# A hybrid decoder trunk on one core: GpSimd's order in the mixing stage, the places of the preparation groups, the order at a stage's first residual, and x and the output in fewer transfers

## What is computed

```python
for l in range(2):
    x = x + 0.5 * swiglu(rmsnorm(x, norm_ffn1[l]), ffn1_w_in[l], ffn1_w_out[l])   # width 2816
    z = rmsnorm(x, norm_mix[l]) @ mix_w_in[l]                                      # 1024 -> 1536
    y_ssm = s5_group(z[:, 0:512], ...)       # diagonal complex state space model, 32 groups
    y_gm = gmlp_group(z[:, 512:1024], z[:, 1024:1536], gm_v_gain[l], gm_w_s[l], gm_b_s[l])
    y = concatenate([rmsnorm(y_ssm, gain_ssm_out[l]), rmsnorm(y_gm, gain_gm_out[l])])
    x = x + y @ mix_w_out[l]
    x = x + 0.5 * swiglu(rmsnorm(x, norm_ffn2[l]), ffn2_w_in[l], ffn2_w_out[l])
return rmsnorm(x, norm_final)
# gmlp_group: u, v = gelu(u), gelu(v); v = rmsnorm of each head of v, times v_gain
#             out = u * (tril(w_s) @ v + b_s), in chunks of 128 tokens
```

## Time and profile before

| | us |
|---|---|
| median of 3 runs | 996.69 (996.29 to 998.61) |
| the profiled execution, its own time | 996.66 |
| its span | 994.9 |
| PE busy in the span | 955.3 |

### The profile page before, as it was taken

The page is one execution under the profiler, slowest core; times in us unless marked ns, Lnnn a source line. Parts: engine busy times, 40 slices in busy tenths (PEclk is TensorE's granted clock), DMA queues, the critical chain, the costliest instruction groups (busy, mean ns, idle before and its releaser), DMA issues.

```text
span 994.9 us, 12027 instructions
## 1 busy us (share of the span) xinstructions
PE 955.3 (96%) x4639; PEld 800.0 (80%) x4639; DVE 553.4 (56%) x619; ACT 470.2 (47%) x670; POOL 391.7 (39%) x611
## 2 busy tenths in 40 slices
PE   5999999999799999999899999999997999999996
PEld 4888888888698888888788888888887888888885
DVE  4556664357657555664256555544684665555543
ACT  5544443456346445443255544443654464544442
POOL 6789998654500788998550000000242000000001
PEclk9999999999899999999799999999997999999999
DMA  9865555344225756554345656555532256556551
GB/s 241 241 199 170 178 197 176 127 130 167 94 77 169 216 178 193 180 191 156 120 126 180 198 177 197 180 187 193 169 127 85 75 180 190 190 169 213 189 169 43
DMA packets 128824, 165.10 MB, mean 166 GB/s; under 512 B 17144, under 2 KB 108416, under 8 KB 128768
## 3 DMA queue, kind: packets, MB, share of 16 engines
q1 hardware_dynamic: 128448, 163.78, 51.8%
q10 hardware_dynamic: 320, 0.56, 0.2%
HBM read 163.27 MB, written 1.05 MB: 165 GB/s over the span
## 4 chain that ended last, share of the span: by engine, by line
PE 57%; POOL 29%; DVE 5%; issue 4%; ACT 2%; SPq 1%; DMA 1%; POOLq 0%; ACTq 0%; DVEq 0%
PE bank L344 16%; PE bank L346 16%; PE bank L345 16%; POOL pt L1080 8%; POOL sc L1080 7%; POOL sc L1083 4%; POOL bp L1080 4%; POOL cw L1086 2%; DVE w_lo L853 1%; PE bank L542 1%; PE bank L585 1%; PE bank L528 1%; PE bank L471 1%; ACT w_hi L647 1%; PE bank L398 1%
## 5 line engine op out<-in xcount | busy, mean ns | idle before, releaser
L853 DVE TENSOR_TENSOR w_lo<-raw,w_hi 128x1024 fp32r<-128x1024 f32 x304 | 383.4, 1265 | 349.6 <-ACT w_hi L647 349.3
L647 ACT ACTIVATE w_hi<-raw 128x1024 fp32r<-128x1024 f32 x304 | 321.2, 1061 | 307.6 <-PE bank L346 301.0
L344 PE MATMUL bank<-w_hi,x_hi 128*128 128x512 f32 x864 | 343.5, 398 | 1.3 <-DVE x_lo L868 1.3
L346 PE MATMUL bank<-w_hi,x_lo 128*128 128x512 f32 x864 | 337.6, 391 | 0.0
L345 PE MATMUL bank<-w_lo,x_hi 128*128 128x512 f32 x864 | 337.0, 390 | 0.0
L346 PEld LDWEIGHTS bank<-w_hi,x_lo 128*128 128x128 f32 x864 | 162.4, 188 | 34.8
L344 PEld LDWEIGHTS bank<-w_hi,x_hi 128*128 128x128 f32 x864 | 162.7, 188 | 33.3 <-issue 1.6
L345 PEld LDWEIGHTS bank<-w_lo,x_hi 128*128 128x128 f32 x864 | 162.9, 188 | 31.9
L1089 POOL TENSOR_TENSOR rstd_c<-ms_c,neg_half 128x2 f32<-128x2 f32 (+1 forms) x8 | 5.8, 724 | 411.4 <-DVE ms_c L873 411.3
L344 PE MATMUL bank<-w_hi,h_hi 128*128 128x512 f32 x352 | 139.4, 396 | 0.0
L345 PE MATMUL bank<-w_lo,h_hi 128*128 128x512 f32 x352 | 137.7, 391 | 0.0
(11 more groups left out here) (137 smaller groups left out, 709.9 us busy)
## 6 DMA issues: line engine op xcount, KB each, us to landing
raw<-in_ffn_w_in SPq DMA_DIRECT2D x174, 512.0 KB
raw<-in_ffn_w_out SPq DMA_DIRECT2D x44, 1024.0 KB
raw<-in_mix_w_in SPq DMA_DIRECT2D x12, 1024.0 KB
raw<-in_mix_w_out SPq DMA_DIRECT2D x8, 1024.0 KB
raw<-in_ffn_w_in SPq DMA_DIRECT2D x4, 256.0 KB, 3.6
x<-in_x SPq DMA_DIRECT2D x6, 128.0 KB, 4.9
out<-x SPq DMA_DIRECT2D x6, 128.0 KB, 2.7
ws_raw<-in_gm_w_s SPq DMA_DIRECT2D x2, 256.0 KB
```

Source lines behind the costliest of these rows:

```text
L344: mm(o, hi_a, hi_b, start=first, stop=False)
L346: return mm(o, lo_a, hi_b, start=False, stop=last)
L647: A(w_hi[:, n % RING, :], raw[:, s, (n % 2) * 1024:(n % 2) * 1024 + 1024], ACT.Copy).then_inc(hi_done, 1)
L853: TT(w_lo[:, n % RING, :], raw[:, s, (n % 2) * 1024:(n % 2) * 1024 + 1024], w_hi[:, n % RING, :].bitcast(F32), ALU.subtract).then_inc(lo_d ...
```

## The change

It reorders instructions on all engines and merges transfers. No arithmetic is added but one split of a small transpose in two; the last scaling of one quarter of x moves from GpSimd and ACT to DVE.

```diff
-GROUP_AT = (9, 12, 15, 18)
+GROUP_AT = ((9, 13, 16, 18), (11, 14, 16, 18))
...
@@ SP: x and the output (xv and ov are views (h, j, n, d) of x and out)
-            for j in range(T):
-                sp.dma_start(x[32 * j:32 * j + 32, 0, :], xv[0, j]).then_inc(x_full[0], 16)
-            for j in range(2):
-                sp.dma_start(x[32 * j:32 * j + 32, 1, :], xv[1, j]).then_inc(x_full[1], 16)
+            for c in range(2):
+                sp.dma_start(x[:, 0, c * 512:c * 512 + 512], xv[0, :, :, c * 512:c * 512 + 512]).then_inc(x_full[c][0], 16)
...
-            for j in range(T):
-                sp.dma_start(ov[0, j], x[32 * j:32 * j + 32, 0, :]).then_inc(stored, 16)
-            sp.wait_ge(fin_done[1], 2)
-            for j in range(2):
-                sp.dma_start(ov[1, j], x[32 * j:32 * j + 32, 1, :]).then_inc(stored, 16)
-            sp.wait_ge(stored, 2 * T * 16)
+            sp.dma_start(ov[0], x[:, 0, :]).then_inc(stored, 16)
+            sp.wait_ge(fin_done[1], 1)
+            sp.dma_start(ov[1, :, :, 0:512], x[:, 1, 0:512]).then_inc(stored, 16)
+            sp.wait_ge(stored, 3 * 16)
...
@@ PE: wide_half, the first block of the first stage
-                    if first_block and kt == 0:
-                        if hh == 0:
-                            x_turn(l, i, 1, 1)
+                    if first_block and kt == 0 and l + i:
+                        x_turn(l, i, 1, 1)
+                if first_block and hh == l + i == 0:
+                    x_turn(l, i, 1, 0)
+                    x_turn(l, i, 1, 1)
...
@@ PE: ffn, after input block b
                         if b == PREP_SMALL[f]:
                             prep_small(f, bank[2 * t1_])
+                        if f == b == 0:
+                            pe.wait_ge(gain_full, 16 * 4)
+                            nc.tensor.transpose(bank[2 * t1_ + 1][:, 0:GAINS], gain_rows,
+                                                ident[0:GAINS, 0:GAINS]).then_inc(gain_t, 1)
+                        if f == 0 and b == 1:
+                            pe.wait_ge(gain_done, 2)
...
-                    if f < DEPTH and k in GROUP_AT:
-                        n = GROUP_AT.index(k)
+                    if f < DEPTH and k in GROUP_AT[f]:
+                        n = GROUP_AT[f].index(k)
...
@@ ACT: first loads
+            act.dma_start(gain_rows[0:KT * DEPTH, :],
+                          a["norm_ffn1"].rearrange("l (t p) -> (l t) p", p=P)).then_inc(gain_first, 16)
+            for c in range(2):
+                act.dma_start(x[:, 1, c * 512:c * 512 + 512], xv[1, :, :, c * 512:c * 512 + 512]).then_inc(x_full[c][1], 16)
...
-            act.wait_ge(xg_done, 1)
-            act.wait_ge(rstd_done, 3 * DEPTH + 2)
-            act.wait_ge(sq_done, 12 * DEPTH + 4)
-            A(x[:, 1, 512:1024], xg, ACT.Copy, scale=rstd_c[:, 1:2]).then_inc(fin_done[1], 1)
             act.wait_ge(fin_done[1], 2)
-            for j in range(2, T):
-                act.dma_start(ov[1, j], x[32 * j:32 * j + 32, 1, :]).then_inc(stored, 16)
+            act.dma_start(ov[1, :, :, 512:1024], x[:, 1, 512:1024]).then_inc(stored, 16)
...
@@ DVE: norm_in; the loops over halves before it end one half earlier
-                    for c, t in ((0, 0), (0, 1), (1, 0)):
-                        residual(before, acc, pairs[c], last_half, c, t, scales[t])
+                    residual(before, acc, pairs[0], last_half, 0, 0, scales[0])
+                    split(l, h + 1)
+                    residual(before, acc, pairs[0], last_half, 0, 1, scales[1])
+                    residual(before, acc, pairs[1], last_half, 1, 0, scales[0])
...
@@ DVE: the last norm
-                if t == 0:
-                    dve.wait_ge(sq_done, 12 * DEPTH + 2)
-                    mean(3 * DEPTH, 0, 1)
-            dve.wait_ge(gfin_full, 16)
-            finish(0, 0)
+                    if c == 1 and t == 0:
+                        dve.wait_ge(sq_done, 12 * DEPTH + 2)
+                        mean(3 * DEPTH, 0, 1)
+                    if c == 0 and t == 1:
+                        finish(0, 0)
+            finish(1, 0)
             dve.wait_ge(sq_done, 12 * DEPTH + 4)
             mean(3 * DEPTH, 1, 2)
-            finish(1, 0)
             finish(0, 1)
+            finish(1, 1)
...
@@ POOL: mix
-                state(1)
                 pool.wait_ge(vms_done, l + 1)
                 inv_sqrt(vrs[:, :], vms[:, :], vrs_done)
-                pool.wait_ge(vrs_done, l + 1)
+                state(1)
+                pool.wait_ge(im_done, l * 2 + 2)
...
@@ POOL: the program's start
-                pool.wait_ge(gain_t, 1)
+                pool.wait_ge(gain_t, 2)
...
+            norm(norm_no(0, 0))
             prep_first(0)
-            norm(norm_no(0, 0))
             prep_rest(0)
```

More of the change, by code:

```diff
@@ L172, in build @@
         first_full = sem("first_full")
-        x_full = [sem("x_full0"), sem("x_full1")]
+        x_full = [[sem(f"x_full{c}{t}") for t in range(2)] for c in range(2)]
+        gain_first = sem("gain_first")
         small_full, c_full, late_full = sem("small_full"), sem("c_full"), sem("late_full")
@@ L243, in load_first @@
             def load_first(w_in, k):
-                src = w_in[0].rearrange("(t p) m -> p t m", p=P)
+                src = w_in[0].rearrange("(t p) (g m) -> p t g m", p=P, g=2)
                 dst = raw[:, 0, :].rearrange("p (t g m) -> p t g m", t=4, g=2)
-                for g in range(2):
-                    sp.dma_start(dst[:, 2 * k:2 * k + 2, g, :],
-                                 src[:, 2 * k:2 * k + 2, g * FF:g * FF + 256]).then_inc((first_full, raw_full[0])[k], 16)
+                for t in range(2 * k, 2 * k + 2):
+                    sp.dma_start(dst[:, t], src[:, t, :, 0:256]).then_inc((first_full, raw_full[0])[k], 16)
             def load_rows(l, c, w, k):
@@ L351, in x_turn @@
                 if l == 0 and i == 0:
-                    pe.wait_ge(x_full[h], 16 * T)
+                    pe.wait_ge(x_full[c][h], 16)
                 else:
@@ L658, in squares @@
                 if l + i == 0:
-                    act.wait_ge(x_full[t], 16 * T)
+                    act.wait_ge(x_full[c][t], 16)
                 else:
@@ L730, in ffn @@
                             prep_small(f, bank[2 * t1_])
+                            if f == 0:
+                                act.wait_ge(gain_t, 2)
+                                A(gains[:, KT * DEPTH:GAINS], bank[2 * t1_ + 1][:, KT * DEPTH:GAINS],
+                                  ACT.Copy).then_inc(gain_done, 1)
                         if h == 4 * PREP_SMALL[f] + 11:
@@ L817, in _ @@
                               a[name].rearrange("l (t p) -> (l t) p", p=P)).then_inc(gain_full, 16)
-            xv = a["x"][0].rearrange("(h n j) d -> h j n d", j=T, n=32)
-            for j in range(2, T):
-                act.dma_start(x[32 * j:32 * j + 32, 1, :], xv[1, j]).then_inc(x_full[1], 16)
             act.wait_ge(gain_t, 1)
-            A(gains[:, :], bank[0][:, 0:GAINS], ACT.Copy).then_inc(gain_done, 1)
+            A(gains[:, 0:KT * DEPTH], bank[0][:, 0:KT * DEPTH], ACT.Copy).then_inc(gain_done, 1)
             act.wait_ge(gain_done, 1)
@@ L920, in ffn @@
                     norm_in(l, 2, UPS[j], ACC_SSM, (ors[:, 2:3], ors[:, 3:4]), OUT + KT - 1)
-                for h in range(4, 4 * UB + FT + 2):
+                for h in range(4, 4 * UB + FT + 1):
                     if h % 4 == 3 and 7 <= h < 7 + 4 * UB:
@@ L1036, in mix @@
                 split(l, UP2)
-                split(l, UP2 + 1)
                 dve.wait_ge(ors_done, l * 2 + 2)
```

21 lines of the change are left out of this document (9 added, 12 removed).

## The result

The changed kernel takes **994.24 us** in the median of 20 runs, against 997.42 us of the kernel before in the same comparison: ratio 0.9945, 95% interval 0.9924 to 0.9965. So it is faster, by 3.2 us in the medians and by 5.5 in the ratio, and not by the 17 that were forecast. Its profiled execution has a span of 993.1 us, against 994.9.

What follows compares the result with a forecast made beforehand. PE is busy 955.3 of 994.9 us, so only its idle 39.6 us and low-clock time can be won. 994.9 -16.8 -8.9 -2.8 +0.7 +5.5 +5.0 = 977.6, plus 1.7 around the span: 979.3 us; range 970 to 991.

Steps and rivals of the forecast that it cites:

- The power ahead: Both mixing stages: GpSimd's power before the states' sums removes PE's waits for `vn` and the low clock behind them, -16.8 us.
- Layer 1's groups: Layer 1's preparation: later group places remove PE's wait for GpSimd's copy and the low clock behind it, -8.9 us.
- rival 3: Another wait replaces that for `vn`, or layer 1's copies exceed their slack: 3 to 8 us back, 983 to 987, chance 0.08.
- Layer 0's groups: Layer 0's preparation: a wait of 0.3 us goes and a new one of 1 comes, +0.7 us.
- The first residual: Five later stages: DVE has the first residual before the last split, so PE's waits for it go, -2.8 us.
- The start: Program start: x over four engines, a new wait for GpSimd's copies behind DVE's mean, and perhaps low clock, +5.5 us.
- The end: Output stores: 256 KB on each of four engines at 24 GB/s takes 10.6 us, +5.0 us.
- rival 2: Four engines at only 14 to 18 GB/s: start +9 to +13, end +8 to +12, 985 to 993 us, chance 0.14.
- The rule of long transfers: Start and end: advice for transfers of 1 MB or more, by which both sides would gain a few us, not cost 6.

Runs made afterwards that it cites:

- p1: Kernel before with only GpSimd's power for v in mixing moved ahead of the products for the states' sums: 982.25 us, ratio 0.9850.
- p2: Kernel before with only the places of the four preparation groups changed, by layer: 991.21 us, ratio 0.9935.
- e1: Changed kernel with x loaded by eight transfers of 32 rows again: 989.81 us, ratio 0.9906 to the kernel before.
- e3: Changed kernel with GpSimd's power of the first norm behind the copies of layer 0's small tables again: 989.38 us, ratio 0.9900 to the kernel before.
- e4: Changed kernel with x and the output each by eight 32-row transfers and the first norm's power behind the copies again: 972.40 us, ratio 0.9743.
- m1: e4 with the half of x on ACT's queue loaded by two four-engine transfers again: 978.30 us, ratio 0.9793 to the kernel before.
- o1: d1 with the output on four engines again, its first half as two transfers of 512 columns, so all packets have 2048 bytes: 979.25 us, ratio 0.9803.
- e2: Changed kernel with the output stored by eight transfers of 32 rows again: 985.60 us, ratio 0.9859 to the kernel before.
- m2: e4 with the half of x on SP's queue loaded by two four-engine transfers again: 974.99 us, ratio 0.9771 to the kernel before.
- d1: e4 with x loaded by 16 transfers of 32 rows and 512 columns, left half first: 970.13 us, ratio 0.9728 to the kernel before.

## Why the prediction was wrong

It was right that the kernel gets faster and wrong by 15 us in how much; the time lies above the range. By its own steps, in the profiled executions:

- **The power ahead**, -16.8: right. It is -15.75, in the two mixing stages of p1, and in those of the changed kernel too once the residual's share is taken off (-16.45 and 0.7). The waits fell to 0.42 us, not to nothing: the forecast gave the power 1.64 us and 0.6 of slack, and it took 2.56. No low clock follows any more.
- **Layer 1's groups**, -8.9: mis-sized, -4.5 (-5.65 less the residual's -1.1). PE came to group 1 when the forecast said, 175.0 us after the stage's start; GpSimd's copy ended at 175.75 and not at 174.1, and the next one came 10.8 us later, not 8.0. So the slack of 0.7 us did not exist, and there are waits of 0.93 and 1.49. The 8.0 us had been read where PE stood waiting, and DVE with it. These are the rows of the kernel before, and then of the changed one:

```profile
484.11 1.71 POOL L1080 TENSOR_TENSOR sc<-sc 128x16 f32<-128x16 f32 x6
486.40 1.28 POOL L1266 COPY w<-bp 64x512 f32<-64x512 f32 x2
487.25 1.51 DVE L853 TENSOR_TENSOR w_lo<-raw,w_hi 128x1024 fp32r<-128x1024 f32 x1 [12.52 <-ACT w_hi L647]
```

```profile
482.82 1.23 DVE L857 TENSOR_TENSOR w_lo<-raw,w_hi 128x1024 fp32r<-128x1024 f32 x1 [1.43 <-ACT w_hi L650]
482.95 2.25 POOL L1273 COPY w<-bp 64x512 f32<-64x512 f32 x2
489.70 2.59 POOL L1087 TENSOR_TENSOR sc<-sc 128x16 f32<-128x16 f32 x6
490.38 1.23 DVE L857 TENSOR_TENSOR w_lo<-raw,w_hi 128x1024 fp32r<-128x1024 f32 x1 [6.33 <-ACT w_hi L650]
485.34 0.84 PE L464 MATMUL bank<-ident,w 128*128 128x128 f32 x6 [0.93 <-POOL w L1273]
495.17 1.06 PE L464 MATMUL bank<-ident,w 128*128 128x128 f32 x8 [1.49 <-POOL w L1273]
```

Before, DVE makes no split for 12.52 us and the same GpSimd steps are short; in the changed kernel each of them that begins within a split is some 0.9 us longer. From this copy to the next one 3 of 16 steps are longer, against none before, and of the 62 steps ahead of it 9 against 7. The forecast's rival 3 has just this (copies later than the slack, since GpSimd's steps vary). The clock falls after the second wait, from 497.6 to 501.0 us; groups 2 and 3 are 9.74 us apart and not 8.18 as in p2, where it stays up, so 1.6 us are lost.
- **Layer 0's groups**, +0.7: the new wait of 1 us did not come, in p2 or in the changed kernel. p2 gives -0.2.
- **The first residual**, -2.8: right. Around the five turns it gives 3.0.
- **The start**, +5.5: mis-sized, and the step with the largest error. It cost 12.8 (4.50 + 7.07, with the residual's 1.1 and layer 0's 0.2 added back). Of these, x over four engines is 5.1 to 5.5 (after against e1, e3 against e4) and the power ahead of the copies 6.1 to 6.5 (after against e3, e1 against e4); the other 1.3 are still there in e4, with the new order of the turns. The forecast had 1.0 for x and the turns together, and 4.5 for the power. The first product came 4.5 us later, not 0.4. Right was that x goes over four engines and that `bs_p` makes a new wait (4.17 for 3.2). The working gave the four engines 24 GB/s each for three queued pieces (whose 32 + 64 + 64 KB are 160, not 192) and let nobody else suffer. What the runs showed: SP stands in its issues for 7.47 us, the next weights and the tables come 8 us late, and meanwhile the sixteen engines are busy for only 0.59 of the time. The low clock after the wait lost some 3 us, more than the upper bound of 2.6. DVE's mean came 4.3 us ahead of PE, even more than the forecast's 3.4, but GpSimd's thirteen copies took 7.25 us, not 5.40:

```profile
28.85 3.60 DVE L857 TENSOR_TENSOR w_lo<-raw,w_hi 128x1024 fp32r<-128x1024 f32 x3 [0.69 <-ACT w_hi L650]
34.36 1.22 DVE L857 TENSOR_TENSOR w_lo<-raw,w_hi 128x1024 fp32r<-128x1024 f32 x1 [0.35 <-ACT w_hi L650]
```

Four splits of DVE ran in that stretch, and four of the thirteen copies took 1.1 to 1.3 us instead of 0.2 or 0.3. In e4 one copy was as long and the thirteen took 4.34 us, before it was two and 5.40, in e3 three and 6.15. The whole trace before says the same: of the GpSimd steps that begin within a split, 103 of 110 are longer than their kind, by 0.9 us in the mean, and of the others 8 of 432. No run moved a split on purpose to try it. The Trainium skill, SBUF — State Buffer, section "SBUF: two separate sides", says that a GpSimd operation that reads SBUF and a VectorE one with two operands in SBUF exclude each other; these rows agree with it.
- **The end**, +5.0: mis-sized, +8.8. The stores began when the forecast said, 1.7 us after the last product (1.8 in the forecast, 3.2 before), which is the 1.4 us that the new order wins; but from the first packet to the last it took 14.2 us and not 10.6. The forecast's figure, 256 KB an engine at 24 GB/s, is the best case. The first half of the output went in 4096-byte packets of 242 ns (17 GB/s an engine); the rate of 24 was reached only once the second transfer was under way, and from 990 us on the DMA share is 0.14, half of that of four engines.

The 15.5 us between forecast and trace are thus 7.3 at the start, 3.8 at the end, 4.4 at layer 1's groups and 1.0 in mixing, less 0.9 for layer 0's groups and 0.2 for the first residual. The step that failed most is the rate and reach of the four-engine transfers, where rival 2 came instead: it gave the start 9 to 13 us and the end 8 to 12, against 12.8 and 8.8 measured, and had a chance of 0.14. Its reason holds only in part, though: it had 14 to 18 GB/s throughout, where the runs show 17 for the first half of the output and 24 for the rest, and at the start stalled issues, and half of the start's cost is the power, not the transfers. Rival 2 alone reached to 993; the time went past it because part of rival 3 came with it, and the range held the two only one at a time. The rule of long transfers, weighed at the end (fewer and larger ones win some us), goes against the measurement here: three stores instead of eight cost 10.2 us. The fixed 2 us that the prediction puts beside it stand in another section of the same page of the Trainium skill (DMA: Bandwidth & Descriptors), "Anatomy of one DMA — SWDGE (gpsimd) path", for transfers that GpSimd issues; none here is.

## What to carry to other kernels

Before transfers are merged, write down the outermost dimension of both sides: in these kernels it gave the number of DMA engines (4 for 4, 8 for 8, 16 for 16 or 32), and a merged pattern of 4 x 32 rows has four. The cost isn't only bytes over fewer engines; issues stall, on the other queue too, and a queue whose issue stalls delays the loads behind it, so look at the issue times of the *small* loads. A step taken ahead of another in an in-order engine (the power ahead of the copies) is to be priced by when its operand comes if all that feeds it is late as well, and by how long the steps behind it take at their new time. And a duration of GpSimd is read together with what DVE does beside it: a chain of steps that was timed while DVE stood still takes longer once the wait that stopped DVE is removed.

## What the hardware showed that was not expected

- Issuing: two transfers of weights took 7.47 us to issue in the kernel after, 1.15 in e1; a table of 8 KB took 4.11 us in m1, 0.50 in e4.
- Four engines moved 26 GB/s in the first two us of the output, then 85 to 102, with 2048-byte packets (o1); with 4096-byte packets 43 to 57 until 984 us (the kernel after). Sixteen moved 240 (e2).
- A GpSimd step that begins within one of DVE's splits lasts some 0.9 us longer: 7.25 us for thirteen copies with four splits, 4.34 with one. The power `vrs` took 1.64 us where DVE stood still and 2.56 where it began within a scan of DVE's of 2.06 us.
- The clock after a wait of 1.5 to 1.7 us for layer 1's second group is not fixed. It was low for 3.4 us in the profiles of the kernel after and of e1 (1.6 us lost), for 6.8 us in those of e2, e3, m1 and m2 (3.2 lost), and not at all in those of e4, d1 and p2, whose waits are as long. Here are m1 and e4 behind that wait, first a stretch of m1 and then one of e4:

```profile
490.00:494.00 4.00, 4.00 (x13) 3.32 (x14) 0.71 (x1) 2.19 (x4) 1.22 (x2) 0.50 0.02 5
```

```profile
486.00:490.00 4.00, 4.00 (x23) 3.41 (x23) 0.93 (x1) 2.51 (x5) 1.23 (x2) 1.00 0.15 52
```

What decides it isn't settled.
